# Two value products of an attention step joined into one matmul of 129 columns, in a hybrid decoder layer on one core

## The chip, the cores and the metric
The kernel runs on one core of a Trainium2 chip. The metric is the device time of one execution in microseconds (us), the median of several runs. A core has five engines: TensorE (PE, with its weight loads shown apart as PEld), VectorE (DVE), ScalarE (ACT), GpSimd (POOL) and SyncE (SP, which here issues the DMAs). Each runs its own instructions in order and waits on semaphores for the others.

## The reference
One layer of a decoder trunk on a prompt of 2048 tokens and on 8 sequences of 4 new tokens, model width 1024. After an RMS norm and one input projection there are three mixers: A, a sliding-window attention (window 128, 4 query heads on 2 key and value heads of 64 channels, with sinks); B, a Mamba-2 scan; C, attention of 4 heads in three branches (window, dilation) of (128, 1), (512, 4) and (2048, 16). Then an output projection and an MLP with squared ReLU. The part that matters here, cut:

```python
def banded_attention(q, k, v, window, dil, table, sink):
    # 128-query blocks; the keys of a block are the previous block and its own
    ...
    logits = jnp.einsum('nbqhgd,nbshd->nbhgqs', qb, kb) + bias
    probs, lse = softmax_with_sink(logits, valid[None, :, None, None], sk)
    out = jnp.einsum('nbhgqs,nbshd->nbqhgd', probs, vb)
```

The kernel keeps p = exp(logits - max) and its row sum, and divides when the branches are joined.

## The kernel before
Every float32 operand of a large product is split in two float16 parts, high and low, and a product is made of three matmuls: high by high, high by low and low by high (`thrice`). After a first stage that normalizes the tokens (until about 330 us), `core` runs one list of units, `units`, which `plan()` writes out and every engine walks in the same order. Its backbone is dense work: `col` (the remaining columns of the input projection, with the convolution on DVE), then for each of four blocks of 512 tokens `out`, `sum`, `up` and `down`. They use the two PSUM banks `dense`. Between these units stand small ones: attention slots (`att`), the scan (`scan`, `sscan`), the joining of branches (`weigh`, `turn`) and the sampled tokens' attention (`sq`, `split`, `sk`, `sx`, `sv`, `se`). They share the six banks `spare`; a table `need`, filled by `claim`, says which semaphore value frees a bank for its next user, and `free` waits for it.

There are 64 real attention tiles (128 queries, 4 heads): 16 of kind 3 (dilation 16), and in each of the four blocks 4 each of kinds 0 (mixer A), 1 and 2. Of these, 42 have a previous block of keys and 22 have none; a tile's key side thus has two halves or one. Some further tiles only load the keys and values of a previous block. A slot `k` works on four tiles at once, one step each:

- PE: `give_values(k - 3)`, `turn_p(k - 2)` (transposes of p, L2379), `score(k - 1)` (L2393), `turn_qk(k)` (transposes, L2405).
- ACT: high part of the transposed p (L1683), high part of q and k (L1688), exponentials (L1695).
- DVE: results of tile `k - 3` from bank 5 to the tile `o` (L1902, L1903; `o_ready`), bias and maximum (L1919 to L1926; it first waits for the scores, L1916), low part of p (L1938; `lo_ready`), low part of q and k (L1944).
- POOL: `split_v(k)`, the high and low parts of the values (L1536, L1538).
- SP: loads `qkv`, stores `o` to the tensor `sums` when `o_ready` says so; `o` has RO = 4 buffers.

The values stand in two tiles `v_hi` and `v_lo`, RV = 5 slots of 4 heads of 65 columns: 64 channels and a last column of ones (in `v_lo` of zeros). So column 64 of a head's result is the sum of p. `give_values` makes, for each head and half, three matmuls of 65 columns into the head's 65 columns of bank 5: p_hi by v_hi, p_hi by v_lo, p_lo by v_hi. Each has its own weight load, since p is the stationary operand.

In the sampled attention, `sk` (L2528) claims banks 4 and 5, and `sv` bank 5; bank 5 is free on `o_ready`, bank 4 on `lo_ready`. Line L2424 is a step of the scan's set-up (`dt`), also in bank 5.

Of the kernel before, what the change touches and what calls it, by code (L numbers as in the profile page):

```python
# [14 lines left out]
F16 = mybir.dt.float16  # L15
BF16 = mybir.dt.bfloat16

P = 128
# [6 lines left out]
HD = 64  # L25
# [692 lines left out]
def core(nc, io, before):  # L718

    with ExitStack() as ctx:  # L720
        a = Alloc(nc, ctx, "core", before)
# [17 lines left out]
        h = a.sb("h", [P, KT, BW])  # L739
# [16 lines left out]
        with ExitStack() as early:  # L756
            soft = early.enter_context(nc.sbuf_tensor("core_soft", [P, 10 * P], F32))
        halves = a.sb("halves", [P, 2, 10 * P], F16)
# [22 lines left out]
        RQ, RK, RV, RO = 3, 3, 5, 4  # L781
        bias = a.sb("bias", [P, 3, 4, 2 * P])
        qkv = a.sb("qkv", [P, RQ, 768])
        qk_t = a.sb("qk_t", [P, RK, 2, 4, P], F16)
        v_hi = a.sb("v_hi", [P, RV, 4, HD + 1], F16)
        v_lo = a.sb("v_lo", [P, RV, 4, HD + 1], F16)
        p = a.sb("p", [P, 4, 2 * P])
        p_hi = a.sb("p_hi", [P, 8, P], F16)
        p_lo = a.sb("p_lo", [P, 8, P], F16)
# [3 lines left out]
        turned, qk_hi, qk_ready, vh_ready, v_ready, s_done, top, maxed, neg_ready, p_ready, p_turned, hi_ready, lo_ready, o_done, o_ready = (  # L793
            a.sem(s) for s in ("turned", "qk_hi", "qk_ready", "vh_ready", "v_ready", "s_done", "top", "maxed", "neg_ready", "p_ready", "p_turned", "hi_ready",
                               "lo_ready", "o_done", "o_ready"))


        A_, NACUM, DT, DT_END, DECAY = range(5)
# [376 lines left out]
        with nc.Block() as block:  # L1175
# [338 lines left out]
            def _(pool):  # L1514
# [1 line left out]
                pool.memset(dt_x[:, NT, :], 0.0).then_inc(ss_pool, 1)  # L1516
                pool.memset(ones[:, :], 1.0).then_inc(made, 1)
                pool.memset(eps[:, :], EPS).then_inc(made, 1)
                pool.memset(v_hi[:, :, :, HD], 1.0).then_inc(made, 1)
                pool.memset(v_lo[:, :, :, HD], 0.0).then_inc(made, 1)  # L1520
                pool.memset(state[:, 0, :], 0.0).then_inc(made, 1)
                pool.memset(conv_raw[:, :, 0:3], 0.0).then_inc(halo_set, 1)
                pool.wait_ge(taps_in, 32)
# [3 lines left out]
                def split_v(n):  # L1527
                    kind, _, _, real, _ = att[n]
                    pool.wait_ge(qkv_in[n % RQ], 16 * (n // RQ + 1))
                    if n >= RV:  # L1530
                        pool.wait_ge(o_done, real_no[n - RV + 2])
                    c0, w = (384, 128) if kind == 0 else (512, 256)
                    nh = w // HD
                    v = qkv[:, n % RQ, c0:c0 + w].rearrange("p (h d) -> p h d", d=HD)
                    hi, lo = (t[:, n % RV, 0:nh, 0:HD] for t in (v_hi, v_lo))
                    pool.tensor_tensor(hi, v, ones[:, 0:w].rearrange("p (h d) -> p h d", d=HD), ALU.mult).then_inc(vh_ready, 1)  # L1536
                    pool.wait_ge(vh_ready, n + 1)
                    pool.tensor_tensor(lo, v, hi, ALU.subtract).then_inc(v_ready, 1)  # L1538
# [292 lines left out]
            def _(dve):  # L1831
# [65 lines left out]
                def attention(first, end, k):  # L1897
                    if first <= k - 3 < end and att[k - 3][3]:
                        e = real_no[k - 3]
                        dve.wait_ge(o_done, e + 1)  # L1900
                        got = spare[5][:, 0:4 * (HD + 1)].rearrange("p (h d) -> p h d", d=HD + 1)
                        dve.tensor_copy(o[:, e % RO, 0:256].rearrange("p (h d) -> p h d", d=HD), got[:, :, 0:HD])  # L1902
                        dve.tensor_copy(o[:, e % RO, 260:264], got[:, :, HD]).then_inc(o_ready, 1)  # L1903
                    if first <= k - 1 < end and att[k - 1][3]:
                        n = k - 1
                        kind, _, _, _, prev = att[n]
                        e = real_no[n]
                        cols = slice(0, 2 * P) if prev else slice(P, 2 * P)
                        if kind == 0:
                            dve.wait_ge(const_in, 64)  # L1910
                        dve.wait_ge(bias_in[BIAS_SLOT[kind]], 32 if kind == 0 else 16)
                        dve.wait_ge(s_done, e + 1)
                        if e >= 1:
                            dve.wait_ge(p_turned, 2 * e)
                        if e >= RO:
                            dve.wait_ge(o_out[e % RO], 16 * (e // RO))  # L1916
                        for hh in range(4):
                            *_, bank, at = place(kind, hh)
                            last = dve.tensor_tensor_reduce(p[:, hh, cols], spare[1 + bank][:, :].rearrange("p (a c) -> p a c", c=2 * P)[:, at, cols],  # L1919
                                                            bias[:, BIAS_SLOT[kind], hh, cols], 1.0, NEG, ALU.add, ALU.max, o[:, e % RO, 256 + hh:257 + hh])  # L1920
                        last.then_inc(top, 1)
                        dve.wait_ge(top, e + 1)
                        if kind == 0:
                            dve.tensor_tensor(o[:, e % RO, 256:260], o[:, e % RO, 256:260], sink[:, :], ALU.max).then_inc(maxed, 1)
                            dve.wait_ge(maxed, kind0_no[n] + 1)
                        dve.tensor_scalar(neg[:, :], o[:, e % RO, 256:260], -1.0, None, ALU.mult).then_inc(neg_ready, 1)  # L1926
                    if first <= k - 2 < end and att[k - 2][3]:
                        n = k - 2
                        e = real_no[n]
                        for half in range(2):  # L1930
                            dve.wait_ge(hi_ready, 2 * e + half + 1)
                            if att[n][4]:
                                src = spare[3 + half][:, :]
                                dst, hi = (t[:, 4 * half:4 * half + 4, :].rearrange("p a c -> p (a c)") for t in (p_lo, p_hi))
                            else:
                                src = spare[3 + half][:, :].rearrange("p (a c) -> p a c", c=P)[:, 1::2, :]
                                dst, hi = (t[:, 4 * half + 1:4 * half + 4:2, :] for t in (p_lo, p_hi))
                            dve.tensor_tensor(dst, src, hi, ALU.subtract).then_inc(lo_ready, 1)  # L1938
# [322 lines left out]
            def _(pe):  # L2261
# [93 lines left out]
                def give_values(n):  # L2355
                    kind, _, _, _, prev = att[n]
                    e = real_no[n]
                    pe.wait_ge(v_ready, n + 1)
                    pe.wait_ge(lo_ready, 2 * e + 2)
                    free(pe, "O", n)  # L2360
                    halves = (0, 1) if prev else (1,)
                    for hh in range(4):
                        kv = place(kind, hh)[3] // HD
                        for half in halves:
                            slot = (n if half else n - 1) % RV
                            for j, (ps, vs) in enumerate(((p_hi, v_hi), (p_hi, v_lo), (p_lo, v_hi))):
                                last = pe.matmul(spare[5][:, hh * (HD + 1):(hh + 1) * (HD + 1)], ps[:, 2 * hh + half, :], vs[:, slot, kv, :],  # L2367
                                                 start=half == halves[0] and j == 0, stop=half == 1 and j == 2)
                    last.then_inc(o_done, 1)

                def turn_p(n):
# [384 lines left out]
```

## Time and profile before

| | |
|---|---|
| median of 3 runs | 2590.69 us (2584.81 to 2594.91) |
| span of the profiled execution | 2593.0 us |
| its own time | not given apart from the span; it is one execution beside the runs above |
| PE busy | 2439.2 us, 94% |
| PEld busy | 1425.9 us, 55% |
| DVE busy | 1232.8 us, 48% |
| ACT busy | 846.8 us, 33% |
| POOL busy | 276.3 us, 11% |

Times in the profile are counted from the start of the span. A busy PE is a union of records; matmuls overlap in their pipeline, so how many fit in a stretch is read from the distance between starts, not from a record's duration. PEclk is the granted clock as a share of 2.4 GHz. The chain that ended last is followed back from the last instruction: at each step to what released it, or to the instruction before it on its engine.

### The profile page before, as it was taken

The numbers are of one execution on the slowest core, as the hardware profiler recorded it, in microseconds if no ns is written. First come the engines' busy times: TensorE is split into PE (matmuls) and PEld (weight loads), VectorE is DVE, ScalarE is ACT, GpSimd is POOL, SyncE is SP. The second block draws the span as 40 slices with busy tenths as digits, with TensorE's granted clock in tenths as the row PEclk, the third lists the DMA queues.
The fourth block names the chain that finished last, engine by engine and source line by source line (L and its number), as shares of the span: only waits on it lengthen the run. The fifth ranks groups of instructions, "written<-read, shape, count | busy, mean of one in ns | idle before, by whom it ended". The sixth has DMA issues, their size and how long they took to land.

```text
span 2593.0 us, 43197 instructions
## 1 busy us (share of the span) xinstructions
PE 2439.2 (94%) x17509; PEld 1425.9 (55%) x17509; DVE 1232.8 (48%) x2843; ACT 846.8 (33%) x1533; POOL 276.3 (11%) x305
## 2 busy tenths in 40 slices
PE   7899879999998999999889999988999999899999
PEld 4455436455444555444455554435555446688887
DVE  3455455566646767742544554125566521322222
ACT  4443244464435443331433231114332111301210
POOL 0111212011101211000111100011101001000000
PEclk9999998899999999999889999999999999999999
DMA  6544363565584667775334555533444544222222
GB/s 210 179 149 163 126 228 117 193 210 176 178 248 155 216 202 227 250 257 183 110 127 140 163 160 156 170 102 125 154 160 162 169 151 134 78 98 91 98 98 80
DMA packets 327588, 414.44 MB, mean 160 GB/s; under 512 B 62111, under 2 KB 248095, under 8 KB 327136
## 3 DMA queue, kind: packets, MB, share of 16 engines
q1 hardware_dynamic: 327392, 411.69, 48.6%
q8 instruction: 140, 2.29, 0.4%
q14 instruction: 56, 0.46, 0.1%
HBM read 300.00 MB, written 111.62 MB: 159 GB/s over the span
## 4 chain that ended last, share of the span: by engine, by line
PE 74%; DVE 6%; ACT 3%; issue 2%; DMA 1%; SPq 1%; POOL 0%; POOLq 0%; DVEq 0%; ACTq 0%
PE core_dense L2279 64%; PE core_spare L2379 2%; PE core_spare L2393 1%; PE core_spare L2367 1%; PE core_spare L2405 1%; PE core_spare L2528 1%; DVE core_col L1993 1%; DVE core_h L1887 1%; DVE core_p L1919 1%; ACT core_p L1695 1%; PE core_spare L2522 1%; PE core_spare L2508 0%; PE core_spare L2462 0%; DVE core_r L1875 0%; PE core_spare L2509 0%
## 5 line engine op out<-in xcount | busy, mean ns | idle before, releaser
L2279 PE MATMUL core_dense<-core_u,core_ring 128*128 128x512 f16 (+2 forms) x4800 | 878.5, 344 | 30.0 <-DVE core_u L1860 16.5
L2279 PEld LDWEIGHTS core_dense<-core_u,core_ring 128*128 128x128 f16 x4800 | 470.3, 99 | 412.2 <-issue 59.6
L2279 PE MATMUL core_dense<-core_r_hi,core_ring 128*128 128x512 f16 (+2 forms) x2560 | 651.5, 340 | 2.6 <-DVE core_h L1887 2.5
L2279 PE MATMUL core_dense<-core_r_lo,core_ring 128*128 128x512 f16 (+2 forms) x1280 | 435.4, 340 | 0.0
L2279 PEld LDWEIGHTS core_dense<-core_r_hi,core_ring 128*128 128x128 f16 x2560 | 251.0, 98 | 198.7 <-issue 7.5
L2279 PE MATMUL core_dense<-tok_u,core_ring 128*128 128x512 f16 x1152 | 271.9, 393 | 17.0 <-DMA core_ring<-scratch_kept_w 17.0
L1887 DVE SCALAR_TENSOR_TENSOR core_h<-core_dense,core_h 128x512 f32<-128x512 f32 (+2 forms) x160 | 94.3, 590 | 341.7 <-PE core_dense L2279 341.4
L1660 ACT ACTIVATE core_r<-core_dense 128x512 f32<-128x512 f32 (+2 forms) x160 | 82.5, 515 | 530.8 <-PE core_dense L2279 530.8
L1875 DVE TENSOR_TENSOR core_r<-core_r 128x512 f32<-128x512 f32 (+2 forms) x160 | 96.1, 601 | 324.4 <-ACT core_r L1660 324.0
L628 PE MATMUL tok_prod<-tok_w_hi,tok_u 128*128 128x512 f16 (+1 forms) x768 | 199.8, 350 | 0.0
L2279 PEld LDWEIGHTS core_dense<-tok_u,core_ring 128*128 128x128 f16 x1152 | 115.4, 101 | 152.1 <-issue 21.5
L2279 PEld LDWEIGHTS core_dense<-core_r_lo,core_ring 128*128 128x128 f16 x1280 | 125.5, 98 | 93.9 <-issue 1.6
L628 PE MATMUL tok_prod<-tok_w_lo,tok_u 128*128 128x512 f16 (+1 forms) x384 | 133.9, 349 | 0.0
L1695 ACT ACTIVATE core_p<-core_p,core_neg 128x256 f32<-128x256 f32 (+1 forms) x256 | 99.7, 461 | 97.1 <-DVE core_neg L1926 96.7
L1837 DVE SCALAR_TENSOR_TENSOR core_ring<-core_staged,core_ring 128x1024 f16<-128x1024 f32 x72 | 90.3, 1254 | 66.4 <-ACT core_ring L1595 65.2
L1536 POOL TENSOR_TENSOR core_v_hi<-core_qkv,core_ones 128x256 f16<-128x256 f32 (+1 forms) x82 | 59.2, 722 | 504.5 <-PE core_spare L2367 256.1
L628 PEld LDWEIGHTS tok_prod<-tok_w_hi,tok_u 128*128 128x128 f16 x768 | 74.8, 99 | 65.7 <-issue 6.7
L1572 POOL TENSOR_TENSOR core_ssum<-core_ssum,core_r 128x512 f32<-128x512 f32 (+1 forms) x28 | 35.9, 1284 | 676.0 <-ACT core_r L1640 676.0
L1878 DVE TENSOR_TENSOR core_r_lo<-core_r,core_r_hi 128x512 f16<-128x512 f32 (+2 forms) x160 | 99.3, 620 | 17.4 <-DVE core_r L1875 0.9
L1993 DVE SCALAR_TENSOR_TENSOR core_col<-core_conv_raw,core_cw,core_col 128x512 f32<-128x512 f32 x96 | 75.1, 782 | 54.0 <-ACT core_conv_raw L1615 51.8
L1919 DVE CUSTOM_DVE_ANT_0 core_p<-core_spare,core_bias 128x256 f32<-128x256 f32 (+1 forms) x256 | 81.4, 372 | 24.7 <-PE core_spare L2393 19.9
L1851 DVE SCALAR_TENSOR_TENSOR core_h<-core_dense,core_x 128x512 f32<-128x512 f32 (+2 forms) x40 | 23.6, 591 | 139.1 <-PE core_dense L2279 139.1
(300 smaller groups left out, 2711.0 us busy)
## 6 DMA issues: line engine op xcount, KB each, us to landing
core_ring<-scratch_kept_w SPq DMA_DIRECT2D x264, 512.0 KB, 4.1
scratch_kept_w<-core_ring SPq DMA_DIRECT2D x72, 512.0 KB, 5.4
core_qkv<-out_tok SPq DMA_DIRECT2D x48, 384.0 KB, 5.6
core_staged<-in_w_up SPq DMA_DIRECT2D x32, 512.0 KB, 4.7
core_staged<-in_w_down SPq DMA_DIRECT2D x32, 512.0 KB, 5.4
out_tok<-tok_tok SPq DMA_DIRECT2D x16, 644.0 KB, 3.0
core_piece<-in_c_kt SPq DMA_DIRECT2D x32, 288.0 KB, 3.8
core_piece<-in_c_v SPq DMA_DIRECT2D x16, 576.0 KB, 4.5
```

The source lines that it names most:

```text
L628: last = pe.matmul(bank[0:nt, 0:w], l, r[:, k, c0:c0 + w], start=k == 0 and i == 0, stop=k == KT - 1 and i == 2, skip_group_check=True)
L1536: pool.tensor_tensor(hi, v, ones[:, 0:w].rearrange("p (h d) -> p h d", d=HD), ALU.mult).then_inc(vh_ready, 1)
L1660: act.activation(r[:, n % 2, 0:w], bank_of["up", b, f, q][:, 0:w], ACT.Relu, scale=1.0 / (WS * HS)).then_inc(r_ready, 1)
L1695: last = act.activation(p[:, hh, cols], p[:, hh, cols], ACT.Exp, bias=neg[:, hh:hh + 1])
L1837: dve.scalar_tensor_tensor(ring[:, q % R, :, 1, :], w_raw[n % RW], WS, ring[:, q % R, :, 0, :], ALU.mult, ALU.subtract).then_inc(lo_split, 1)
L1875: dve.tensor_tensor(r2[:, n % 2, 0:w], r[:, n % 2, 0:w], r[:, n % 2, 0:w], ALU.mult).then_inc(r2_ready, 1)
L1878: dve.tensor_tensor(r_lo[:, f % HF, off:off + w], r2[:, n % 2, 0:w], r_hi[:, f % HF, off:off + w], ALU.subtract).then_inc(rl_ready, 1)
L1887: dve.scalar_tensor_tensor(here, bank_of["down", b, i, q][:, 0:w], HS * HS / WS, here, ALU.mult, ALU.add).then_inc(down_added, 1)
L1919: last = dve.tensor_tensor_reduce(p[:, hh, cols], spare[1 + bank][:, :].rearrange("p (a c) -> p a c", c=2 * P)[:, at, cols], bias[:, BIAS_ ...
L1993: dve.scalar_tensor_tensor(dst, conv_raw[:, i, j:j + 512], cw[:, i, j:j + 1], dst, ALU.mult, ALU.add).then_inc(tap, 1)
L2279: ins = pe.matmul(bank, w[:, k, part, :], s, start=first and j == 0, stop=last and j == 2, skip_group_check=True)
L2379: last = pe.transpose(spare[3 + b][:, at:at + P], p[:, 2 * b + hh, half * P:(half + 1) * P], ident[:, :])
```

## The change
`v_hi` and `v_lo` become one tile `v_all` with 130 columns a head: 64 high channels, a one, 64 low channels, a zero. For heads 0 to 2, one matmul of 129 columns takes p_hi past both; its result has 64 columns of high parts, the row sum and 64 columns of low parts, 129 columns of bank 5 for a head. A matmul of 65 columns adds p_lo by the high values. Head 3 would not fit in the bank's 512 columns that way (4 x 129 = 516) and keeps its three matmuls, of 65, 64 and 65 columns. The low parts of heads 0 to 2 are now added by DVE: where it had two copies it has four copies and an addition, with a wait on a new semaphore `o_high` in front of the addition. The diff, without the two changed memsets in POOL's opening:

```diff
-        v_hi = a.sb("v_hi", [P, RV, 4, HD + 1], F16)
-        v_lo = a.sb("v_lo", [P, RV, 4, HD + 1], F16)
+        VW, VL = 2 * HD + 2, HD + 1
+        v_all = a.sb("v_all", [P, RV, 4, VW], F16)
...
-                    hi, lo = (t[:, n % RV, 0:nh, 0:HD] for t in (v_hi, v_lo))
+                    hi, lo = (v_all[:, n % RV, 0:nh, at:at + HD] for at in (0, VL))
...
-                        got = spare[5][:, 0:4 * (HD + 1)].rearrange("p (h d) -> p h d", d=HD + 1)
-                        dve.tensor_copy(o[:, e % RO, 0:256].rearrange("p (h d) -> p h d", d=HD), got[:, :, 0:HD])
-                        dve.tensor_copy(o[:, e % RO, 260:264], got[:, :, HD]).then_inc(o_ready, 1)
+                        got = spare[5][:, 0:3 * (VW - 1)].rearrange("p (h d) -> p h d", d=VW - 1)
+                        three = o[:, e % RO, 0:192].rearrange("p (h d) -> p h d", d=HD)
+                        dve.tensor_copy(three, got[:, :, 0:HD]).then_inc(o_high, 1)
+                        dve.tensor_copy(o[:, e % RO, 260:263], got[:, :, HD])
+                        dve.tensor_copy(o[:, e % RO, 192:256], spare[5][:, 3 * (VW - 1):3 * (VW - 1) + HD])
+                        dve.tensor_copy(o[:, e % RO, 263:264], spare[5][:, 3 * (VW - 1) + HD:3 * (VW - 1) + VL])
+                        dve.wait_ge(o_high, e + 1)
+                        dve.tensor_tensor(three, three, got[:, :, VL:VL + HD], ALU.add).then_inc(o_ready, 1)
...
-                            for j, (ps, vs) in enumerate(((p_hi, v_hi), (p_hi, v_lo), (p_lo, v_hi))):
-                                last = pe.matmul(spare[5][:, hh * (HD + 1):(hh + 1) * (HD + 1)], ps[:, 2 * hh + half, :], vs[:, slot, kv, :],
-                                                 start=half == halves[0] and j == 0, stop=half == 1 and j == 2)
+                            at = hh * (VW - 1)
+                            here, first = v_all[:, slot, kv, :], half == halves[0]
+                            if hh < 3:
+                                pe.matmul(spare[5][:, at:at + VW - 1], p_hi[:, 2 * hh + half, :], here[:, 0:VW - 1], start=first, stop=False, skip_group_check=True)
+                            else:
+                                pe.matmul(spare[5][:, at:at + VL], p_hi[:, 2 * hh + half, :], here[:, 0:VL], start=first, stop=False, skip_group_check=True)
+                                pe.matmul(spare[5][:, at:at + HD], p_hi[:, 2 * hh + half, :], here[:, VL:VL + HD], start=False, stop=False, skip_group_check=True)
+                            last = pe.matmul(spare[5][:, at:at + VL], p_lo[:, 2 * hh + half, :], here[:, 0:VL], start=False, stop=half == 1, skip_group_check=True)
```

## Rows read from the trace of the kernel before
**Rows 1.** The page's engine table: busy us (share of the span), instructions.
```profile
PE 2439.2 (94%) x17509; PEld 1425.9 (55%) x17509; DVE 1232.8 (48%) x2843; ACT 846.8 (33%) x1533; POOL 276.3 (11%) x305
```
**Rows 2.** The page's slices, 40 of 65 us: busy and granted clock in tenths.
```profile
PE   7899879999998999999889999988999999899999
...
PEclk9999998899999999999889999999999999999999
```
**Rows 3.** The page's chain that ended last, shares by engine and by line.
```profile
PE 74%; DVE 6%; ACT 3%; issue 2%; DMA 1%; SPq 1%; POOL 0%; POOLq 0%; DVEq 0%; ACTq 0%
PE core_dense L2279 64%; PE core_spare L2379 2%; PE core_spare L2393 1%; PE core_spare L2367 1%; PE core_spare L2405 1%; PE core_spare L2528 1%; DVE core_col L1993 1%; DVE core_h L1887 1%; DVE core_p L1919 1%; ACT core_p L1695 1%; PE core_spare L2522 1%; PE core_spare L2508 0%; PE core_spare L2462 0%; DVE core_r L1875 0%; PE core_spare L2509 0%
```
**Rows 4.** Stretches (A:B, length): busy us of each engine, clock, DMA share, GB/s.
```profile
340.00:510.00 170.00, 153.28 (x1134) 89.88 (x1131) 94.85 (x335) 74.83 (x169) 32.23 (x47) 0.91 0.53 181
820.00:950.00 130.00, 130.00 (x1139) 75.65 (x1138) 90.14 (x216) 69.71 (x126) 24.68 (x28) 1.00 0.61 203
```
**Rows 5.** The value tile's instructions: duration ns min/median/max, first and last start.
```profile
L2367 PEld LDWEIGHTS core_spare<-core_v_hi,core_p_hi x424: 95/97/151, 356.0 to 1904.2; 128*128 128x128 f16 x142
L2367 PE MATMUL core_spare<-core_v_hi,core_p_hi x424: 190/193/262, 356.3 to 1904.2; 128*128 128x65 f16 x142
```
**Rows 6.** PE's timeline, one value step of 24: start, duration, what.
```profile
1285.19 0.19 PE L2367 MATMUL core_spare<-core_v_hi,core_p_hi 128*128 128x65 f16 x1
...
1285.89 0.19 PE L2367 MATMUL core_spare<-core_v_hi,core_p_lo 128*128 128x65 f16 x1
```
**Rows 7.** The chain, 1285 to 1300 us: start, us on the chain, what.
```profile
1285.35 0.73 PE core_spare L2367 x24
...
1288.24 5.20 PE core_dense L2279 x24
...
1295.90 0.09 DVE core_o L1902
...
1296.38 0.33 DVE core_p L1919
...
1298.15 1.20 DVE core_p_lo L1938 x2
...
1299.60 1.05 PE core_spare L2528 x65
```
**Rows 8.** A stretch of 0.8 us (columns of rows 4), and PE's timeline in it.
```profile
432.60:433.40 0.80, 0.80 (x14) 0.80 (x13) 0.00 (x0) 0.60 (x1) 0.80 (x1) 0.50 0.00 0
...
432.63 0.25 PE L2367 MATMUL core_spare<-core_v_lo,core_p_hi 128*128 128x65 f16 x1
...
433.18 0.24 PE L2367 MATMUL core_spare<-core_v_hi,core_p_lo 128*128 128x65 f16 x1
```
**Rows 9.** DVE's timeline, a tile's results.
```profile
1288.53 0.41 DVE L1902 COPY core_o<-core_spare 128x256 f32<-128x256 f32 x1
1288.86 0.14 DVE L1903 COPY core_o<-core_spare 128x4 f32<-128x4 f32 x1
1288.93 0.41 DVE L1919 CUSTOM_DVE_ANT_0 core_p<-core_spare,core_bias 128x256 f32<-128x256 f32 x1
```
**Rows 10.** The chain from 360 us, tiles of 128 keys.
```profile
360.49 0.42 DVE core_o L1902
...
360.98 0.20 DVE core_p L1919
```
**Rows 11.** DVE's timeline, small copies.
```profile
1355.84 0.17 DVE L2195 COPY core_dt_all<-core_spare 128x8 f32<-128x8 f32 x1 [0.53 <-PE core_spare L2528]
1355.92 0.16 DVE L2196 COPY core_dt_all<-core_spare 128x12 f32<-128x12 f32 x1
```
**Rows 12.** DVE's timeline: idle time in a slot after the copies (in brackets).
```profile
1324.66 0.42 DVE L1919 CUSTOM_DVE_ANT_0 core_p<-core_spare,core_bias 128x256 f32<-128x256 f32 x1 [1.06 <-PE core_spare L2393]
...
1353.42 1.29 DVE L1938 TENSOR_TENSOR core_p_lo<-core_spare,core_p_hi 128x512 f16<-128x512 f32 x2 [0.60 <-ACT core_p_hi L1683]
```
**Rows 13.** The chain near 1891 us.
```profile
1891.38 0.42 DVE core_o L1902
```

More of the change, by code:

```diff
@@ L795, in core @@
                                "lo_ready", "o_done", "o_ready"))
+        o_high = a.sem("o_high")
         A_, NACUM, DT, DT_END, DECAY = range(5)
@@ L1518, in _ @@
                 pool.memset(eps[:, :], EPS).then_inc(made, 1)
-                pool.memset(v_hi[:, :, :, HD], 1.0).then_inc(made, 1)
-                pool.memset(v_lo[:, :, :, HD], 0.0).then_inc(made, 1)
+                pool.memset(v_all[:, :, :, HD], 1.0).then_inc(made, 1)
+                pool.memset(v_all[:, :, :, VW - 1], 0.0).then_inc(made, 1)
                 pool.memset(state[:, 0, :], 0.0).then_inc(made, 1)
```

## The prediction
> **What bounds the kernel now.** I read the page's engine table first [rows 1]: PE is busy 94% of a span of 2593.0 us, DVE 48%. A microsecond taken off PE's queue can therefore be a microsecond won, while one added to DVE costs only where PE, or what PE waits for, stands behind it. The slices of 65 us [rows 2] show PE at nine tenths or more except in slices 1, 2, 5, 6, 13, 20, 21, 27, 28 and 35; the granted clock falls to eight tenths in slices 7 and 8 (390 to 520 us) and 20 and 21 (1230 to 1360 us), where small attention and scan work stands between the dense products. The chain that ended last [rows 3] is 74% PE and 6% DVE; of it the dense products (L2279) are 64% and the value products this change touches (L2367) 1%, some 26 to 39 us. So the stake on PE is the packing of that one per cent; the stake on DVE is how often its own time stands in the chain.
>
> The stretch table [rows 4] says where DVE could matter: from 340 to 510 us PE is busy 153.28 of 170 us at a mean clock of 0.91, so it is often kept waiting; from 820 to 950 us it is busy all 130.00 us, and there DVE at 90.14 of 130 us has slack.
>
> **PE's part.** There are three groups of 424 value matmuls (high p by high v, high p by low v, low p by high v), one of them shown [rows 5]: 106 tile halves times 4 heads (42 attention tiles have a previous block and 22 don't, 2 x 42 + 22 = 106), 1272 in all. After, heads 0 to 2 issue two matmuls in a half instead of three, head 3 still three: 106 x (3 x 2 + 3) = 954. So 318 matmuls and their weight loads go.
>
> But the columns don't go. A head's half streamed 3 x 65 = 195 columns, and now 129 + 65 = 194. What can be won is only what a matmul costs beyond its columns. The 24 value matmuls at 1285 us start 0.70 us apart from first to last, 23 intervals, 30.4 ns each [rows 6]; 24 dense matmuls of 512 columns take 5.20 us of the chain, 216.7 ns each [rows 7]. The line through both is 0.417 ns per column (one column a cycle at 2.4 GHz) plus 3.3 ns. A matmul of 129 columns then costs 57.1 ns, a head's half 57.1 + 30.4 = 87.5 ns for 91.2, a gain of 3.7 ns; times 318 that is 1.2 us. Bounds: if a narrow matmul's 30.4 ns were partly a floor, and a 129-column one cost its columns alone (53.8 ns), the gain is 7.0 ns x 318 = 2.2 us; if it cost twice 30.4 ns, nothing is gained. I take 1.2 us, since both measured widths lie on one line. At the lower clock the intervals are longer but their excess over the columns isn't: in a stretch with a granted clock of 0.50, that is the 1.2 GHz level [rows 8], the value matmuls start 55 ns apart (ten intervals in 0.55 us; 65 columns at 1.2 GHz are 54.2 ns), so no more is won there.
>
> The removed weight loads last 97 ns each in the records [rows 5], which would make 318 x 97 ns = 31 us if they stood in line. They don't: 24 load-matmul pairs fit in 0.73 us, so each load runs under the matmuls ahead of it.
>
> The Trainium skill (TensorE: Matmul & The Clock Gate, Back-to-back issue gap) speaks for more: it says that in a stream of load and matmul pairs the spacing is set by both, and gives about 81 ns per matmul at 128 columns against some 56 ns for the matmul alone. By that a load would cost about 25 ns and the estimate of the gain be 318 x 25 ns = 8 us; the row disagrees, since pairs of 65 columns start 30.4 ns apart.
>
> **DVE's part.** Before, the results of a tile leave PSUM in two copies, of 4 x 64 and of 4 elements a partition. They start 0.33 us apart, and the next operation 0.07 us later [rows 9]: 0.40 us in all. After, there are five operations: a copy of 3 x 64, one of 3, one of 64, one of 1, and an addition of 3 x 64 with one operand in PSUM. The prices: an operation of DVE that reads PSUM occupies it for 0.20 us at 128 elements [rows 10], 0.33 at 256 and 0.60 at 512 (two L1938 in 1.20 us) [rows 7], two operands or one; very small copies from PSUM start 0.08 us apart [rows 11]. By the line between them 192 elements cost 0.27 us and 64 cost 0.14. The sum is 0.27 + 0.08 + 0.14 + 0.08 + 0.27 = 0.84 us, so 0.44 us more for a tile, and 64 x 0.44 = 28 us more of DVE's busy time. The new wait on o_high is for a copy that three others follow; that copy has long ended, so it costs nothing of its own. Bounds: were every one of the five exposed for its whole recorded duration (0.35 + 0.15 + 0.21 + 0.15 + 0.35 us, interpolated from the same rows) against 0.41 + 0.14, the addition is 0.66 us; were the two tiny copies free, it is 0.28 us.
>
> A rule of the Trainium skill (VectorE: DVE Perf Modes, the errata section) prices an operation from PSUM at 120 cycles of 0.96 GHz plus its elements. Estimated by it, three more operations and 256 more elements add 0.64 us to a tile, the upper bound's size; the rows show less because a following operation starts before the earlier one's record ends (0.33 us after the start of a copy that lasts 0.41).
>
> Where does it lie? attention() on DVE puts these operations first in the slot, ahead of the four L1919 reductions, the negated maximum, the split of p and low_qk, so all are late by 0.44 us, with ACT's exponentials behind them; SP's store of o waits on o_ready too, but 4 buffers cover it. In most slots this is hidden: there DVE next waits on something that takes longer, as 1.06 us on PE's scores or 0.60 us on ACT's split [rows 12], or PE has a dense group of 5.2 us still ahead of it. In ten of the 64 slots L1902 is itself on the chain: five from 360.49 us [rows 10] to 401.79, two, at 1295.90 [rows 7] and 1422.51, and three from 1779.80 to 1891.38 [rows 13]. At 1295.90 one sees how it reaches PE: copies, reductions, split of p (L1938), and then PE's sampled score product L2528, which needs PSUM bank 4. Ten times 0.44 is 4.4 us; bounds 2.8 us (0.28) and 6.6 us (0.66). POOL writes the same elements to other addresses, with the same number of instructions and waits: zero, covered by its 11% load. The two memsets change only their column: zero.
>
> **Sum.** 4.4 - 1.2 = +3.2 us; from the bounds +0.6 (2.8 - 2.2) to +6.6 us (6.6 - 0). The profiled execution is given by its span of 2593.0 us alone, 2.3 us over the median of 2590.69 and inside the three runs (2584.81 to 2594.91), so the difference carries over to the median unchanged: 2593.9 us. Half a per cent is 13 us, about what a measurement of this kernel can tell from no change.
>
> **Rivals.**
> (a) The loads do stand in line in part, by some 25 ns each in stretches where PE's queue runs dry, or the recorded starts are too kind. Then up to 318 x 25 ns = 8 us are won on PE, and with 4.4 us lost on DVE it ends at 2587 us; the time could be 2583 us if DVE's part is hidden too. For it: the 97 ns records. Against it: 30.4 ns from start to start.
> (b) DVE's lateness is exposed almost everywhere and not only in the ten slots: another 0.44 us moves slots that now have less slack than that onto the chain. All 64 exposed give 28.2 us, less 1.2: 2618 us. The point from which it decides is 13 us, that is 32 slots. For it: the 16 slots of the stretch 340 to 510 us, where DVE's convolution, ACT and PE already take turns in the chain. Against it: from 510 to 960 us L1902 isn't once on the chain, and the slack rows are larger than 0.44 us.
> (c) PE's added idle moments bring further drops to the 1.2 GHz level in the stretches with a clock below one. A drop such as that at 432 us makes 24 dense matmuls of 5.2 us take twice that; three or four more partly at the lower clock would add some 5 to 10 us, 2599 to 2604 us. The same can fall the other way by chance, by a few us.
> (d) The change does nothing that can be told: the mean of what I forecast lies there anyway.
> The Trainium skill (TensorE: Matmul & The Clock Gate, Part 1) says too that idleness lowers the clock to 1.2 GHz, and the 0.50 and 0.91 of the rows agree; it gives (c) no price that the rows don't.
>
> **How the numbers follow.** The forecast with (d), that is between +0 and +7 us: 0.66. (a): 0.10. (b), in part or whole: 0.10, of which half crosses 13 us. (c): 0.14, of which a fifth crosses it together with a part of (b). Faster by over 0.5% needs 13 us, more than (a) gives: 0.03. Slower by over 0.5%: 0.05 + 0.03 and a little for operations of DVE that are dearer than their rows, 0.09. Within: 0.88. The range runs from 2582 us (case (a) with DVE's part hidden, rounded down by 1 us) to 2605 us (the far end of (c)); the likeliest case's own is 2590 to 2598 us.
>
> **What would show it.** In the profile after: 954 value matmuls, 318 of them 129 columns wide, starting about 57 ns and then 30 ns apart; the 24-matmul step of 0.73 us turned into 18 matmuls in 0.70. DVE busy near 1261 us for 1232.8, with the five operations taking 0.84 us from the first copy to the next L1919. The idle before L2528 at 1296 us longer by 0.4 us, and no change of PE's idle from 820 to 950 us. I am wrong if the 129-column matmuls start under 45 ns apart, if the stretch from 510 to 950 us changes by more than 2 us, or if the granted clock of the stretch 340 to 510 us moves by more than 0.03.

## The result and the profile after

The changed kernel takes 2594.61 us (median of 20 runs, 2589.36 to 2603.02) against 2590.65 us of the kernel before (20 runs, 2582.87 to 2594.91). The ratio is 1.0021, with a 95% interval of 1.0011 to 1.0031: slower by 5.4 us (2.8 to 8.0) by the ratio and 4.0 us by the medians, within half a per cent. The forecast was 2593.9 us, slower by 3.2. Two runs far above all others of their kernels, one of the 12 of dve_alone below (13203.53 us) and one of the 27 of the kernel before in the last series (3024.69 us), are left out of every median and ratio.

The page of the kernel after has these rows for engines and granted clock, and under them its two stretches that answer to [rows 4] (a different query, same columns):

```profile
PE 2441.8 (94%) x17191; PEld 1428.1 (55%) x17191; DVE 1258.6 (48%) x3035; ACT 845.5 (33%) x1533; POOL 276.9 (11%) x305
...
PEclk9999988899999999999889999999999999999999
```
```profile
340.00:510.00 170.00, 154.28 (x1084) 91.99 (x1082) 99.42 (x375) 73.61 (x164) 32.09 (x45) 0.90 0.52 177
...
820.00:950.00 130.00, 129.55 (x1087) 75.49 (x1085) 94.62 (x253) 69.29 (x127) 26.18 (x30) 1.00 0.61 204
```

PE has 318 matmuls fewer and DVE 192 operations more than in [rows 1]. DVE's busy time rose by 25.8 us, PE's didn't fall. The value tile's instructions of the kernel after (columns of [rows 5]) are the 954 that were counted:

```profile
L2379 PE MATMUL core_spare<-core_v_all,core_p_lo x424: 191/192/262, 357.5 to 1910.8; 128*128 128x65 f16 x142
...
L2375 PE MATMUL core_spare<-core_v_all,core_p_hi x318: 217/220/315, 357.4 to 1910.5; 128*128 128x129 f16 x159
...
L2377 PE MATMUL core_spare<-core_v_all,core_p_hi x106: 192/193/246, 357.7 to 1910.7; 128*128 128x65 f16 x106
...
L2378 PE MATMUL core_spare<-core_v_all,core_p_hi x106: 193/195/243, 357.7 to 1910.8; 128*128 128x64 f16 x106
```

PE's timeline in one step of 18, where [rows 6] has a step of 24:

```profile
1289.32 0.22 PE L2375 MATMUL core_spare<-core_v_all,core_p_hi 128*128 128x129 f16 x1
1289.38 0.19 PE L2379 MATMUL core_spare<-core_v_all,core_p_lo 128*128 128x65 f16 x1
1289.41 0.22 PE L2375 MATMUL core_spare<-core_v_all,core_p_hi 128*128 128x129 f16 x1
...
1290.00 0.19 PE L2379 MATMUL core_spare<-core_v_all,core_p_lo 128*128 128x65 f16 x1
1290.03 0.30 PE L2390 MATMUL core_spare<-core_ident,core_p 128*128 128x128 f32 x1
```

A wide matmul holds PE for some 60 ns and a narrow one for 30, and from the first to the transposes behind (L2390) the step takes 0.71 us; the same distance in the step of [rows 6] is 0.73 us. The six pairs of heads 0 to 2 start within 0.53 us (1289.32 to 1289.85), 88 ns a pair, against 91 ns for the three matmuls they replace. DVE's timeline for one tile's results, where [rows 9] has two copies in 0.40 us:

```profile
1292.67 0.34 DVE L1904 COPY core_o<-core_spare 128x192 f32<-128x192 f32 x1
1292.94 0.14 DVE L1905 COPY core_o<-core_spare 128x3 f32<-128x3 f32 x1
1293.01 0.21 DVE L1906 COPY core_o<-core_spare 128x64 f32<-128x64 f32 x1
1293.14 0.14 DVE L1907 COPY core_o<-core_spare 128x1 f32<-128x1 f32 x1
1293.20 0.34 DVE L1909 TENSOR_TENSOR core_o<-core_o,core_spare 128x192 f32<-128x192 f32 x1
1293.46 0.41 DVE L1925 CUSTOM_DVE_ANT_0 core_p<-core_spare,core_bias 128x256 f32<-128x256 f32 x1
```

That is 0.27, 0.07, 0.13, 0.06 and 0.26 us from start to start, 0.79 us in all, 0.39 us more than before. The chain of the kernel after shows where it counts, at the place of [rows 7]:

```profile
1300.21 0.27 DVE core_o L1904
...
1300.67 0.33 DVE core_o L1909
1301.00 0.33 DVE core_p L1925
...
1302.78 1.20 DVE core_p_lo L1944 x2
...
1304.22 1.05 PE core_spare L2539 x65
```

All of DVE's results, reductions and splits stand between the dense group and the sampled score product (L2539, before L2528). PE sat idle for 3.93 us in front of that product, and for 3.39 us in the profile of [rows 7]: 0.54 us more, where 0.4 was forecast.

### The profile page after: what moved, and what is told of

Same layout as the page of the kernel before. It is cut to its first block, busy times and chain, and to the rows that moved or that the text cites. A ratio compares the mean times of both kernels' runs of the same rounds, so it can differ in the third digit from the quotient of the medians.

```text
span 2599.6 us, 42753 instructions
## 1 busy us (share of the span) xinstructions
PE 2441.8 (94%) x17191; PEld 1428.1 (55%) x17191; DVE 1258.6 (48%) x3035; ACT 845.5 (33%) x1533; POOL 276.9 (11%) x305
## 4 chain that ended last, share of the span: by engine, by line
PE 74%; DVE 6%; ACT 3%; issue 2%; DMA 1%; SPq 1%; POOL 0%; POOLq 0%; DVEq 0%; ACTq 0%
PE core_dense L2285 63%; PE core_spare L2390 2%; PE core_spare L2404 1%; PE core_spare L2416 1%; PE core_spare L2539 1%; DVE core_col L1999 1%; DVE core_h L1888 1%; DVE core_p L1925 1%; ACT core_p L1696 1%; PE core_spare L2375 1%; PE core_spare L2533 1%; PE core_spare L2519 0%; PE core_spare L2473 0%; DVE core_r L1876 0%; PE core_spare L2520 0%
## 5 line engine op out<-in xcount | busy, mean ns | idle before, releaser
L1537 POOL TENSOR_TENSOR core_v_all<-core_qkv,core_ones 128x256 f16<-128x256 f32 (+1 forms) x82 | 59.8, 730 | 506.3 <-PE core_spare L2379 270.5
```

## Experiments

The comparison with the kernel before is by ratio in each; its median was 2590 to 2592 us in all three series, so 0.1% is 2.6 us.

**Two controls.** The kernel before and the kernel after, unchanged.

> The kernel before, unchanged, as another kernel in the comparison: it shows what two executions of one program differ by. Expected: a ratio within 0.2% of 1, and a second profile whose stretches differ from the first one's by a few us, with the granted clock.

> The change, unchanged, on the chip of the other three: before + 4 us again (2 to 6), and a second profile in which what belongs to the change (value steps of 710 ns, 0.79 us of DVE a tile, DVE busy near 1259 us) is as in the first, while the places of the lower clock differ.

before_again: 2590.69 us, ratio 1.0002 (0.9991 to 1.0013). after_again: 2594.08 us, ratio 1.0016 (1.0007 to 1.0025), the loss again. Each also gave a second profile, and these two (spans of 2588.4 and 2591.9 us) are the better pair to compare: the profiled runs lie within 0.4 us of their kernels' medians, where that of the kernel after (2601.39 us) lay 7 above its own. PE's timelines of before_again and after_again, with PE's idle time in front in brackets, at two places of the last attention stretch:

```profile
1777.56 0.63 PE L2576 MATMUL core_spare<-core_ident,core_soft 128*128 128x128 f32 x4 [1.67 <-DVE core_o L1919]
...
1878.49 0.65 PE L2528 MATMUL core_spare<-core_pt,core_halves 128*128 128x16 f16 x19 [0.37 <-DVE core_halves L2190]
```
```profile
1778.16 0.63 PE L2587 MATMUL core_spare<-core_ident,core_soft 128*128 128x128 f32 x4 [2.08 <-DVE core_o L1925]
...
1881.52 0.94 PE L2539 MATMUL core_spare<-core_pt,core_halves 128*128 128x16 f16 x30 [1.16 <-DVE core_halves L2196]
```

The first wait grew by 0.41 us, about one tile's added time, and so did a third, behind these two (0.83 and 1.25 us, in the rows further down). The second grew by 0.79. Of that only one tile's time is the change's. The rest comes from an operation of DVE ahead of the results, the low part of the MLP's activations `r`, and from what POOL did beside it. DVE's and POOL's timelines, of before_again and then of after_again:

```profile
1871.21 0.69 DVE L1878 TENSOR_TENSOR core_r_lo<-core_r,core_r_hi 128x512 f16<-128x512 f32 x1
1871.38 1.12 POOL L1536 TENSOR_TENSOR core_v_hi<-core_qkv,core_ones 128x256 f16<-128x256 f32 x1 [11.89 <-DMA core_qkv<-out_tok]
```
```profile
1873.27 0.73 POOL L1537 TENSOR_TENSOR core_v_all<-core_qkv,core_ones 128x256 f16<-128x256 f32 x1 [10.59 <-DMA core_qkv<-out_tok]
1873.34 1.21 DVE L1879 TENSOR_TENSOR core_r_lo<-core_r,core_r_hi 128x512 f16<-128x512 f32 x1
```

Where POOL's operation started first, DVE's took 1.21 us for 0.69; the row has POOL's start wait for a DMA. In the first profile of the kernel after DVE's took 0.69 us, and there the same wait of PE is 0.79 us, 0.42 more than 0.37. In all of them DVE had been idle for 4.64 us shortly before, so no lateness of an earlier slot is in it.

The granted clock differs there too. The stretch from 1770 to 1800 us, of before_again and then of after_again (columns of [rows 4]):

```profile
1770.00:1800.00 30.00, 26.93 (x238) 15.65 (x237) 18.90 (x56) 13.94 (x29) 6.31 (x6) 0.94 0.27 91
```
```profile
1770.00:1800.00 30.00, 26.53 (x211) 15.13 (x210) 18.70 (x63) 13.88 (x29) 6.38 (x6) 0.89 0.22 75
```

A mean of 0.89 for 0.94 in 30 us is 3 us more at the 1.2 GHz level, some 1.5 us lost. The dense group behind the first wait shows it directly:

```profile
1779.92 6.46 PE L2279 MATMUL core_dense<-core_u,core_ring 128*128 128x512 f16 x24
```
```profile
1780.52 8.03 PE L2285 MATMUL core_dense<-core_u,core_ring 128*128 128x512 f16 x24
```

Seven profiles agree. After a first wait of 1.66 to 1.68 us (before, before_again, pe_alone) the group took 6.46 to 6.64 us and the mean clock was 0.94; after one of 2.01 to 2.08 (after, after_again, dve_alone, three_ops) it took 7.94 to 8.03 us at 0.89. That isn't in proportion to the wait: in act_takes and before_late (below), with a first wait of 1.37 us, the group took 7.03 and 6.54 us. The whole stretch, from the transposes at its start to the third wait, in before_again and in after_again:

```profile
1751.85 0.87 PE L2405 MATMUL core_spare<-core_ident,core_qkv 128*128 128x128 f32 x3 [2.42 <-DVE core_soft L2150]
...
1893.13 0.87 PE L2528 MATMUL core_spare<-core_pt,core_halves 128*128 128x8 f16 x27 [0.83 <-DVE core_halves L2190]
```
```profile
1751.93 0.87 PE L2416 MATMUL core_spare<-core_ident,core_qkv 128*128 128x128 f32 x3 [2.42 <-DVE core_soft L2156]
...
1896.55 0.86 PE L2539 MATMUL core_spare<-core_pt,core_halves 128*128 128x8 f16 x27 [1.25 <-DVE core_halves L2196]
```

That is 141.28 and 144.62 us from start to start. It was 141.79 in before and 141.22 in pe_alone, and 144.05, 144.38 and 144.02 in after, dve_alone and three_ops: every kernel with more work on DVE loses 2.2 to 3.4 us in this one stretch.

A longer wait isn't always a loss. In front of the product at 1294.60 us of before_again PE was idle for 3.18 us, in after_again for 3.92; but the 24 dense matmuls behind took 7.96 us in the one and 7.46 in the other, and between the transposes ahead of and behind both (1289.20 to 1304.11 us, and 1289.85 to 1304.96) only 0.20 us of the 0.74 are left.

**One half at a time.** dve_alone leaves PE and the bank as before and gives DVE the five operations:

```diff
-                        dve.tensor_copy(o[:, e % RO, 0:256].rearrange("p (h d) -> p h d", d=HD), got[:, :, 0:HD])
-                        dve.tensor_copy(o[:, e % RO, 260:264], got[:, :, HD]).then_inc(o_ready, 1)
+                        three = o[:, e % RO, 0:192].rearrange("p (h d) -> p h d", d=HD)
+                        dve.tensor_copy(three, got[:, 0:3, 0:HD]).then_inc(o_high, 1)
+                        dve.tensor_copy(o[:, e % RO, 260:263], got[:, 0:3, HD])
+                        dve.tensor_copy(o[:, e % RO, 192:256], got[:, 3, 0:HD])
+                        dve.tensor_copy(o[:, e % RO, 263:264], got[:, 3, HD:HD + 1])
+                        dve.wait_ge(o_high, e + 1)
+                        dve.tensor_tensor(three, three, got[:, 0:3, 0:HD], ALU.max).then_inc(o_ready, 1)
```

> PE and the bank's layout as before; DVE alone takes the five operations of the change (copies of 3 x 64, 3, 64 and 1 elements, the wait, and a two-operand operation of 3 x 64, here the maximum of the copied values with themselves, which changes nothing). Theory (DVE's lateness is exposed in about ten slots): 0.39 us more for a tile, so before + 4 to 5 us, nearly all of it before 450 us and between 1740 and 1910 us, and nothing between 510 and 1250 us. Rival 1 (DVE exposed everywhere): before + 25 us. Rival 2 (the joined matmuls cause the loss): before + 0.

pe_alone is the change with two copies on DVE, the first with `bass.AP(rows.tensor, rows.offset, [list(rows.ap[0]), [VW - 1, 4], [1, HD]])` as its source:

> The joined matmuls of the change, but DVE makes two copies as before (4 x 64 at a stride of 129, and 4 sums); the low parts of heads 0 to 2 are left out of the output. Theory: before - 1.2 us, steps of 24 matmuls (732 ns to the next work) turned into 18 (710 ns). Rival 1 (weight loads stand in line by 25 ns each): before - 8 us. Rival 2 (a wide matmul costs two narrow ones, or more): before + 0 or slower.

dve_alone: 2597.09 us (11 runs), ratio 1.0026 (1.0016 to 1.0037), +6.7 us (4.1 to 9.6). pe_alone: 2588.18 us, ratio 0.9993 (0.9980 to 1.0006), -1.8 us (-5.2 to +1.6). Together +4.9 us, which is the change's loss: it comes from DVE, and PE's gain is small. The rivals in which loads stand in line (-8 us), in which DVE is exposed everywhere (+25) or in which the wide matmuls are the loss (dve_alone at 0) are outside the intervals.

**PE's part enlarged.** One run alone can't tell 1.2 us from nothing, so the value steps were issued five times in two kernels:

```diff
-                    for hh in range(4):
-                        kv = place(kind, hh)[3] // HD
+                    for _ in range(5):
+                        for hh in range(4):
+                            kv = place(kind, hh)[3] // HD
```

> The kernel before, with every value step's matmuls issued five times (each pass starts the accumulation anew, so the output is unchanged). Theory: four more passes of 1272 matmuls at 30.4 ns: 155 us of PE's time, less what fits in PE's idle moments: before + 140 to 155 us. It is there to be compared with pe_alone_x5.

> The joined matmuls with DVE's two copies (low parts of heads 0 to 2 left out of the output), and every value step's matmuls issued five times. Theory: a step costs 3.7 ns less for each of 318 joined pairs and pass, 5 x 1.2 = 6 us less than before_x5. Rival (weight loads in line by 25 ns): 40 us less. Rival (a 129-column matmul costs two of 65): 0.

before_x5: 2724.46 us, ratio 1.0519 (1.0497 to 1.0540), +134 us, under the 140 to 155 expected; which idle moments took the rest wasn't followed. pe_alone_x5: 2713.87 us, ratio 1.0482 (1.0461 to 1.0502). The difference is 10.6 us by the medians and 9.6 by the ratios, where 6 was expected, and the intervals leave several us each way. The chain of before_x5 and then of pe_alone_x5 has one step each:

```profile
863.27 3.67 PE core_spare L2368 x120
866.94 0.91 PE core_spare L2380 x8
```
```profile
868.59 0.06 PE core_spare L2371
868.68 0.06 PE core_spare L2371
...
872.12 0.91 PE core_spare L2386 x8
```

90 matmuls take 3.53 us (868.59 to 872.12) where 120 take 3.67: 0.14 us in a fivefold step with both halves. Taking half of that for a step with one half, this is 42 x 0.14 + 22 x 0.07 = 7.4 us of PE's own time in the whole kernel, 1.5 us for a single pass. Where the rest of the 10 us lies isn't shown. The 40 us of loads in line are refuted.

**DVE's part enlarged.** In dve_fourfold the two-operand operation of dve_alone stands four times, in a chain:

```diff
+                        dve.wait_ge(o_high, 4 * e + 2)
+                        dve.tensor_tensor(three, three, got[:, 0:3, 0:HD], ALU.max).then_inc(o_high, 1)
+                        ...
```

> As dve_alone, with the last two-operand operation done four times, each waiting for the one before it: some 1.5 us more for a tile than before, 4 times that of the change. Theory (ten slots exposed, others have slack of 0.6 us and more, which this uses up): before + 20 to 35 us, growing faster than in proportion because slots join in. If only the ten slots ever count: + 15 us. If every slot counts: + 96 us.

2636.35 us, ratio 1.0175 (1.0154 to 1.0196), +45 us, more than the 20 to 35 expected. DVE's timeline gives the added time:

```profile
1311.88 0.34 DVE L1904 COPY core_o<-core_spare 128x192 f32<-128x192 f32 x1
...
1313.83 0.42 DVE L1931 CUSTOM_DVE_ANT_0 core_p<-core_spare,core_bias 128x256 f32<-128x256 f32 x1
```

1.95 us for 0.40, 1.55 more. As if exposed in 29 of 64 slots (45 / 1.55), where dve_alone's 6.7 / 0.39 is as if in 17. These are not counts of slots: the clock's part is in them (1.5 us of dve_alone's 6.7 at 1780 us alone; here the mean granted clock of the four runs was 0.968 for 0.972, up to 10 us). That slots join in as their slack goes is likely but not shown, and even here it isn't all of them.

**Another place or another engine.** before_late and after_late move DVE's block, with its wait on `o_done`, behind the line that makes `neg` in the same slot:

```diff
                         dve.tensor_scalar(neg[:, :], o[:, e % RO, 256:260], -1.0, None, ALU.mult).then_inc(neg_ready, 1)
+                    if first <= k - 3 < end and att[k - 3][3]:
+                        e = real_no[k - 3]
+                        dve.wait_ge(o_done, e + 1)
+                        ...
```

> The kernel before, with DVE's two result copies moved behind the reductions and the negated maximum of the same slot, so that they no longer delay ACT's exponentials, but o_ready comes 1.0 to 1.6 us later. Theory (their place ahead in the slot is what makes DVE's time count): 0.40 us won in the slots whose chain runs through the exponentials (four or five), and lost again where bank 5 is wanted next (dt at 389 us, the sv slots): before - 2 to + 2 us. Rival (the place doesn't matter): before + 0 with no stretch changed by over 0.5 us.

> The change, with DVE's five result operations moved behind the reductions and the negated maximum of the same slot. Theory: in the slots whose chain runs through the exponentials 0.79 us is won, in those where bank 5 is wanted next 1 to 1.6 us is lost: the change - 3 to + 2 us. Rival (the place doesn't matter): as the change.

before_late: 2598.15 us, ratio 1.0035 (1.0022 to 1.0048), +9 us. after_late: 2607.54 us, ratio 1.0068 (1.0051 to 1.0086), +18 us. Both expectations failed. The theory behind them held in part: in before_late the three waits of the last stretch that had grown in the change are shorter (1.37 us for 1.67, none for 0.37, 0.43 for 0.83). But the later bank 5 loses more. PE's waits for it, in before_again and then in before_late (us in total, times, longest):

```profile
PE core_spare L2528 <- DVE core_o L1903: 2.0, 1, 2.0
```
```profile
PE core_spare L2528 <- DVE core_o L1926: 5.7, 3, 2.0
```

That is 3.7 us of the 9. The mean granted clock over before_late's 12 runs was 0.9692, over the 29 of the kernel before 0.9716; a mean lower by 0.0024 is 12 us more at 1.2 GHz in 2590 us, up to 6 us lost if PE had work throughout. These two can account for the loss; they weren't separated. In after_late the mean of six runs was 0.9678, for 0.9728 of the kernel before beside it.

act_takes gives the two copies of the kernel before to ACT, ahead of its exponentials; act_joined has the joined matmuls, ACT's copy of the high parts and sums, and DVE's addition behind `neg`:

```diff
+                        act.wait_ge(o_done, e + 1)
+                        act.activation(o[:, e % RO, 0:256].rearrange("p (h d) -> p h d", d=HD), got[:, :, 0:HD], ACT.Copy)
+                        act.activation(o[:, e % RO, 260:264], got[:, :, HD], ACT.Copy).then_inc(o_ready, 1)
```

> The kernel before, with the two result copies of a tile taken by ACT instead of DVE, placed ahead of ACT's exponentials, where ACT mostly waits for DVE's negated maximum. It is the reverse of dve_alone: 0.40 us less of DVE for a tile where dve_alone had 0.39 more. Theory (DVE's time ahead of the reductions is exposed in ten slots or more): before - 4 to - 6 us, in the stretches before 450 us and after 1250 us, provided ACT's copies fit in its wait. Rival 1 (ACT's copies delay the exponentials by as much): before + 0 or slower. Rival 2 (it is only added time that is exposed, because the slots' slack is asymmetric): before - 1 us.

> The joined matmuls, with ACT taking the high parts and sums (a copy of 4 x 64 and one of 4) ahead of its exponentials, and DVE only adding the low parts of three heads, behind its negated maximum. DVE does 0.27 us a tile for 0.40 before and 0.79 in the change, PE's 1.2 us are kept. Theory: before - 2 to - 5 us where exponentials are on the chain, less what bank 5 comes free later for its next users; no faster than act_takes. Rival (the joined matmuls are worth their price once DVE is relieved): clearly under act_takes.

act_takes: 2589.27 us, ratio 1.0003 (0.9991 to 1.0015): no gain, the expected 4 to 6 us are excluded. act_joined: 2600.99 us, ratio 1.0042 (1.0028 to 1.0055), +11 us, also missed. The page of act_takes shows DVE relieved by 26.3 us, and its waits (second and third rows) where that went:

```profile
PE 2432.3 (94%) x17509; PEld 1424.6 (55%) x17509; DVE 1206.5 (47%) x2715; ACT 868.6 (34%) x1661; POOL 276.4 (11%) x305
...
DVE core_p L1919 <- PE core_spare L2393: 54.6, 28, 5.4
...
PE core_spare L2528 <- ACT core_o L1694: 4.3, 4, 1.2
```

DVE now waits 54.6 us for PE's scores; in before_again it was this:

```profile
DVE core_p L1919 <- PE core_spare L2393: 19.4, 21, 1.3
```

And four of PE's sampled products wait for ACT's copy. PE's timeline in the last stretch of act_takes, to be read against that of before_again above:

```profile
1774.00 0.63 PE L2576 MATMUL core_spare<-core_ident,core_soft 128*128 128x128 f32 x4 [1.37 <-DVE core_o L1919]
...
1817.25 0.93 PE L2528 MATMUL core_spare<-core_pt,core_halves 128*128 128x16 f16 x30 [1.12 <-ACT core_o L1694]
...
1891.84 0.87 PE L2528 MATMUL core_spare<-core_pt,core_halves 128*128 128x8 f16 x27 [0.43 <-DVE core_halves L2190]
```

So time taken off DVE shows at the same places as time added to it: the first wait is 1.37 us for 1.67, the one near 1878 us is gone (0.37), the last is 0.43 for 0.83. What ate the gain here is ACT's copy, which frees bank 5 later: PE waits for it for 1.12 us at 1817 us and for 1.23 at 1835, where before_again has no wait. The run thus doesn't tell whether a kernel with less work on DVE, and bank 5 free as early, would win. In act_joined DVE waits besides for ACT's copy (25.4 us, 17 times, by its waits) before it can free bank 5, and PE's sampled products wait 7.4 us, in four places, for DVE's addition.

**Fewer operations.** three_ops is the change with one copy of 4 x 64 at a stride of 129, one of the four sums at that stride, and the addition.

> The change, but with one copy of 4 x 64 at a stride of 129 and one of the 4 sums, then the addition of 3 x 64: three operations for five. Theory: 0.33 + 0.07 + 0.27 = 0.67 us a tile for 0.79, so 0.12 x 10 = 1.2 us less than the change: before + 3 us. Rival (the number of operations and their fixed cost is what counts): half of the loss gone, before + 2 us.

2595.71 us, ratio 1.0020 (1.0007 to 1.0033), +5.2 us. This is the change's own ratio; neither 1.2 us nor the rival's gain can be told from it. In its profile the three operations take 0.73 us at 1874.73 us, for the 0.67 of the theory. An addition with both operands in PSUM, which would need no first copy, wasn't tried.

No version beat the kernel before.

## Why the prediction was right

**The columns stay, only what a matmul costs besides goes.** Right: a step of 24 matmuls in 0.73 us became one of 18 in 0.71, 88 ns a pair for the 87.5 forecast. The gain of 1.2 us on PE is inside pe_alone's interval (-5.2 to +1.6), and the fivefold step's rows give 1.5 us. Case (a), loads in line by 25 ns, is refuted by both: 97 ns is how long a load is under way, not what it takes of PE.

**DVE's price.** 0.84 us a tile forecast from the rows for 64 to 512 elements and the tiny copies, 0.79 measured; 0.44 us more forecast, 0.39 measured; DVE busy 1261 us forecast, 1258.6 measured. The wait on `o_high` costs nothing that the rows show (0.06 us from L1907 to L1909). The Trainium skill's price for an operation from PSUM (VectorE: DVE Perf Modes, the errata section) is above what these rows show. The prediction worked out 0.64 us from it with 256 more elements for a tile; the five operations have 452 and the two had 260, 192 more, so the estimate by that page is 0.58 us. Nothing in the sum used it.

**Where it is exposed.** The ten slots on the chain were the right kind of place: the first profile of the kernel after has ten of them on its chain too, and the waits at 1777, 1878 and 1893 us each grew by one tile's added time (0.41, 0.42 in the first profile, 0.42), and the chain at 1300 shows the path that the prediction named. But the term was undersized, if the middle of the interval is taken: dve_alone costs 6.7 us (4.1 to 9.6) where the term was 4.4 with bounds of 2.8 and 6.6. What the sum left out is the clock: it priced a slot by DVE's added time alone. In the last stretch three slots had 1.3 us in the sum and lost 2.2 to 3.4, since the dense group behind the first longer wait ran some 1.5 us longer at the lower clock, in all four profiles with more work on DVE and in none of the three without. So rival (c), which the prediction set against its forecast, is in part an addition to it. The other way round, of a wait longer by 0.74 us near 1295 us only 0.20 stayed. What each of the other slots cost stays open. Between 340 and 450 us more time at the lower clock came in some profiles only. The chain of the kernel after has, behind the slot at 404 us,

```profile
408.74 3.55 PE core_spare L2459 x16
```

and that of the kernel before, for the same 16 matmuls (L2448),

```profile
405.77 1.90 PE core_spare L2448 x16
```

with a granted clock of 0.50 in the stretch 408.5 to 412.5 us of the one and of 1.00 in 405.7 to 407.7 us of the other. It isn't a constant of the change: over all runs the mean clock was 0.9716 both for the kernel before (29 runs) and for the one after (20), and 0.9718 for dve_alone (11). A loss of 1.5 us would move such a mean by 0.0006, about as much as it is uncertain.

**The sum.** +3.2 us forecast; 4.0 by the medians. That it came so near is partly luck: by dve_alone DVE's term was some 2 us too small, and PE's, by the fivefold step and pe_alone, 0.3 to 0.6 us. The prediction's step from the span to the median took the profiled execution to lie 2.3 us above the median; a run's time is some 1.9 us over its span (2601.39 and 2599.6 us for the profiled run of the kernel after), so it lay some 4 us above. The difference, which alone was carried over, isn't touched.

**The rivals.** (b), all 64 slots, didn't come: from the first dense group behind 510 us to one near 934 us the change added 1.1 us in the first pair of profiles (512.19 to 933.65 us before, 515.53 to 938.04 after) and -0.2 in the second (510.25 to 932.33, 507.95 to 929.80), within the 2 us that the prediction allowed. dve_fourfold shows that even at four times the added time the loss is that of 29 slots and not of 64. The granted clock from 340 to 510 us was 0.90 for 0.91, within the 0.03 allowed. (d) can't be told from the forecast by one run, but the interval (2.8 to 8.0 us) excludes that nothing happened.

## What to carry to other kernels

Joining two matmuls that stream past the same stationary operand saves only what a matmul costs beyond its columns, here 3 to 4 ns each, if the trace shows starts at one column a cycle; read the distance between starts, not the records' durations. Any added result operation on the engine that empties PSUM must be priced against that: here three more small operations of DVE, 0.39 us a tile, outweighed 318 removed matmuls several times over. And a wait has to be priced with the clock behind it: where PE waited 0.4 us longer, the group behind ran 1.5 us longer at the lower clock in one place, and won part of the wait back in another. Work moved to another engine brings that engine's own lateness: in act_takes the waits for DVE shrank as they should, and new ones for ACT took their place.

## What the runs showed of the hardware

- A matmul of 129 columns holds PE for about 58 ns, on the same line as 65 columns (30.4 ns) and 512 (216.7 ns); its weight load is hidden all the same.
- Small operations of DVE that read PSUM start 0.06 to 0.07 us apart even at one element, though each is recorded with 0.14 us.
- ACT took the copy of 4 x 64 and that of 4 elements in records of 0.38 and 0.18 us, about DVE's.
- One operation of DVE from and to SBUF (128x512, float32 to float16, L1878) took at most 0.69 us in each of the 144 to 148 executions, of 160 in a profile, beside which POOL did nothing, and up to 1.21 us in those beside which POOL worked (before, before_again, after, after_again, dve_alone).
- After a wait of PE longer by 0.4 us, the 24 dense matmuls behind took 7.94 to 8.03 us in four profiles, for 6.46 to 6.64 in three, the mean granted clock of 30 us being 0.89 for 0.94. It isn't in proportion: at another place the group behind a longer wait was shorter.
- Two profiles of one program differ by several us in a stretch: the granted clock for 340 to 510 us and its neighbours falls at different places in each. Waits of PE were the same to some 0.2 us in most places; they are the better witness for a change of this size.
